# Sample tile before the prompt tiles, and every second of its v rows summed on VectorE

## The reference, cut to what matters

```python
h = layer_norm(ALPHA * x + token_mixer(x, ...))
# PEER(h): 8 heads x 16 best of 128 x 128 experts, for every token
s1, s2 = q1 @ keys1.T, q2 @ keys2.T         # q = h @ wq
expert, top_s = the 16 best of the sums of the 16 best of s1 and of s2
gate = softmax(top_s)
act  = gelu(einsum('td,thkd->thk', h, u[expert]))
out  = einsum('thk,thkd->td', gate * act, v[expert])
y = layer_norm(ALPHA * h + out)
```

## Time and profile before

| | |
|---|---|
| median of 3 runs | 2185.09 us |
| lowest and highest run | 2184.09 and 2194.29 us |
| span of the profiled execution | 2197.0 us |
| busy: PE, VectorE, ScalarE, GpSimd | 1744.4, 1086.9, 435.3, 843.3 us |
| bytes read, rate over the span | 550.23 MB, 256 GB/s |

### The profile page before, as it was taken

The page is one execution under the profiler, slowest core; times in us unless marked ns, Lnnn a source line. Parts: engine busy times, 40 slices in busy tenths (PEclk is TensorE's granted clock), DMA queues, the critical chain, the costliest instruction groups (busy, mean ns, idle before and its releaser), DMA issues.

```text
span 2197.0 us, 17908 instructions
## 1 busy us (share of the span) xinstructions
PE 1744.4 (79%) x5473; PEld 909.0 (41%) x5473; DVE 1086.9 (49%) x2606; ACT 435.3 (20%) x1031; POOL 843.3 (38%) x840
## 2 busy tenths in 40 slices
PE   7998888899888666787789778777989675766765
PEld 6844565444457222334445334333434222322322
DVE  3516456202147999535553645443142995343452
ACT  1211311201021111130332222114121122112111
POOL 0000000000003665554653554444143667777773
PEclk9999888999999988998889888889999988888888
DMA  6432011433359998996877897879898889999995
GB/s 203 168 137 105 8 70 54 178 134 115 133 171 339 351 315 285 335 375 226 276 267 276 298 314 253 274 264 372 288 388 288 311 311 345 368 361 353 364 363 224
DMA packets 220760, 563.39 MB, mean 256 GB/s; under 512 B 19770, under 2 KB 70394, under 8 KB 220250
## 3 DMA queue, kind: packets, MB, share of 16 engines
q0 software_dynamic: 112352, 408.88, 51.5%
q1 hardware_dynamic: 108050, 152.58, 20.3%
q10 hardware_dynamic: 288, 1.05, 0.1%
HBM read 550.23 MB, written 12.23 MB: 256 GB/s over the span
## 4 chain that ended last, share of the span: by engine, by line
PE 49%; DVE 19%; DMA 12%; issue 9%; POOL 5%; ACT 4%; another core or an unknown queue 1%; POOLq 0%; SPq 0%; DVEq 0%; ACTq 0%
PE bank L792 18%; PE bank L726 7%; PE bank L727 6%; PE bank L833 5%; DVE BIG L1489 4%; DMA wbuf<-in_w_in_dram 4%; ACT BIG L1164 3%; POOL BIG L658 3%; DMA out_s_ssm_dram<-BIG 3%; PE bank L772 2%; POOL BIG L653 2%; DMA BIG<-in_peer_v_dram,small 2%; PE bank L1104 2%; DMA BIG<-in_peer_u_dram,small 2%; DVE BIG L1947 2%
## 5 line engine op out<-in xcount | busy, mean ns | idle before, releaser
L726 PE MATMUL bank<-BIG 128*128 128x512 f32 x768 | 454.9, 677 | 267.5 <-DMA BIG<-in_peer_v_dram,small 117.6
L653 POOL DMA_INDIRECT BIG<-in_peer_u_dram,small x384 | 407.2, 1060 | 475.3 <-DVE small L1489 354.1
L658 POOL DMA_INDIRECT BIG<-in_peer_v_dram,small x384 | 409.1, 1065 | 194.6 <-issue 111.0
L792 PE MATMUL bank<-wbuf,BIG 128*128 128x512 f32 x992 | 435.1, 598 | 12.9 <-DMA wbuf<-in_w_in_dram 7.1
L727 PE MATMUL bank<-BIG 128*128 128x512 f32 x768 | 431.1, 645 | 0.0
L726 PEld LDWEIGHTS bank<-BIG 128*128 128x128 f32 x768 | 156.1, 215 | 488.1 <-issue 424.6
L1489 DVE CUSTOM_DVE_ANT_0 BIG<-BIG 128x1024 f32<-128x1024 f32 x256 | 303.9, 1221 | 14.4 <-DMA BIG<-in_peer_u_dram,small 12.6
L792 PEld LDWEIGHTS bank<-wbuf,BIG 128*128 128x128 f32 x992 | 189.1, 192 | 253.9 <-issue 235.0
L727 PEld LDWEIGHTS bank<-BIG 128*128 128x128 f32 x768 | 162.3, 211 | 216.1 <-issue 216.1
L2021 DVE CUSTOM_DVE_ANT_0 BIG<-BIG 128x1024 f32<-128x1024 f32 x128 | 156.3, 1226 | 182.5 <-DMA BIG<-in_peer_u_dram,small 137.0
L1164 ACT ACTIVATE BIG<-cst,small 128x128 f32<-128x128 f32 x384 | 127.7, 392 | 470.2 <-DVE small L1484 345.1
(11 more groups left out here) (186 smaller groups left out, 1274.8 us busy)
## 6 DMA issues: line engine op xcount, KB each, us to landing
wbuf<-in_w_in_dram SPq DMA_DIRECT2D x24, 2048.0 KB
wbuf<-in_w_in_dram SPq DMA_DIRECT2D x16, 1536.0 KB
wbuf<-in_w_ssm_br_dram SPq DMA_DIRECT2D x8, 2048.0 KB
wbuf<-in_peer_wq_dram SPq DMA_DIRECT2D x8, 2048.0 KB
wbuf<-in_w_attn_br_dram SPq DMA_DIRECT2D x4, 2048.0 KB
wbuf<-in_w_out_dram SPq DMA_DIRECT2D x4, 2048.0 KB
BIG<-in_state_ssm_dram SPq DMA_DIRECT2D x16, 512.0 KB, 6.1
out_s_ssm_dram<-BIG SPq DMA_DIRECT2D x16, 512.0 KB
```

The source lines that it names most:

```text
L653: pool.indirect_dma_start(slot, None, table_u, bass.IndirectOffsetOnAxis(ap=idx, axis=0)).then_inc(u_in[j], 16)
L658: pool.indirect_dma_start(slot, None, table_v, bass.IndirectOffsetOnAxis(ap=idx, axis=0)).then_inc(v_in[j], 16)
L726: mm(acc[0][:, :], dg[:, j, :], slots[j][:, 0:512], start=False, stop=False, skip_group_check=True)
L792: last = mm(dst[:, :], lhs(b, k, toks[t]), wbuf[b][:, k, :], start=(k == 0), stop=(k == KC - 1))
```

## The change

The order of the passes is turned: `ST` comes first, with nothing beside it, and `PR` second, with the 64 ticks of the sample tile's rows beside it (66 with the ends; 57 in the mixer, 8 beside the first pick of tile 0, one after). The rows of both prompt tiles, 2 x 128, then run alone in blocks of eight: 32 blocks instead of 16. The picks of tile 2 are beside the conv of `PR`; the first half of tile 0 is picked after `PR` with ticks beside it, the second half after the ticks, the halves of tile 1 after 4 and after 8 of the 32 blocks.

Of the two v rows of a tick the first stays on TensorE, and VectorE adds the second, times its weight, to a sum `accS` in SBUF (where a table lies that only the state-space part of `ST` reads); at the end the sum is added to the h of tile 2. ScalarE makes one diagonal a tick instead of two. The blocks of eight still use TensorE for all rows.

Also: the early gates are gone, all gates are done in their phase; small DMAs that GpSimd issued for `PR` (outputs, biases, norm weights) are issued by SyncE; the caches' loads come in the first conv; GpSimd reads the expert numbers where they lie, without copies, and its list and most loops are written out; `TICKS_AT` is new; the buffers lie elsewhere in SBUF.

```diff
-PROMPT_BLOCKS = 2 * BLOCKS
-TICKS = PROMPT_BLOCKS + 3
+TICKS = BLOCKS + 2
...
-TICKS_AT = dict(pick=1, conv=1, dt=1, qkv=1, tails=2, rope=1, keys=2, item1=2, item2=1, item3=1, ya=1,
-                select=1, xbt=2, seg=1, state=1, group=1, y=1, z=1, yT=1, ym=0, gates=1, mixedT=1, out=1, hT=1, wq=1,
-                scores=2)
+ORDER = {2: 0, 0: 1, 1: 2}
+
+TICKS_AT = dict(pick=(1,), conv=(1,), dt=(0,), qkv=(1, 0, 1, 1), tails=(0,), rope=(1,), keys=(1,), select=(1,),
+                item1=(0,), item2=(1, 0), item3=(0,), ya=(1,), xbt=(0,), seg=(0,), y=(1,), z=(1,), yT=(1,), ym=(1,),
+                gates=(1,), mixedT=(1,), out=(0, 1), hT=(1,), wq=(1, 0), scores=(0,))
...
             def tick(k):                                  # TensorE
...
-                    for j in range(b % 2 * WB, b % 2 * WB + WB):
-                        expert_rows(diag, v_used, j, vslot, (v_in[j], 16 * (b // 2 + 1)))
+                    j = b % 2 * WB
+                    expert_rows(2, diag, v_used, j, vslot, (v_in[j], 16 * (b // 2 + 1)))
...
-                if not q.streams:
-                    early_gates(0)
...
                 # ScalarE, conv of the second pass
-                        if q.streams and i >= 2 and j % 3 == 2:
+                        if not q.first and i >= 2 and j % 3 == 2:
                             step("pick")
...
             def tick(k):                                  # VectorE
...
+                b = k - 2
+                if b >= 0:
+                    slot = b % 2 * WB + 1
+                    dve.wait_ge(v_in[slot], 16 * (b // 2 + 1))
+                    if b:
+                        dve.wait_ge(v_added, b)
+                        stt(accS, vslot[slot], w8[b % 2][:, 1:2], accS, ALU.mult, ALU.add).then_inc(v_added, 1)
+                    else:
+                        tsc(accS, vslot[slot], w8[b % 2][:, 1:2], None, ALU.mult).then_inc(v_added, 1)
...
             # GpSimd
+            for b in range(BLOCKS + 2):
+                if b == BLOCKS // 2:
+                    pool.wait_ge(idx_ready, 2)
+                if b < BLOCKS:
+                    for j in range(b % 2 * WB, b % 2 * WB + WB):
+                        if b >= 2:
+                            pool.wait_ge(dot_done, WB * (b - 2) + j % WB + 1)
+                        gather(table_u, uslot[j], 2 * P + b * WB + j % WB, u_in[j])
+                c = b - 2
+                if c >= 0:
+                    for j in range(c % 2 * WB, c % 2 * WB + WB):
+                        if c >= 2:
+                            pool.wait_ge((v_used, v_added)[j % WB], c - 1)
+                        gather(table_v, vslot[j], 2 * P + c * WB + j % WB, v_in[j])
...
             # VectorE, the end
+            mixer(ST)
             mixer(PR)
-            mixer(ST)
+            pick(0, 0, lambda place: steps.at("pick"))
             places.append(list(steps.seen))
-            for half in range(2):
-                pick(2, half, lambda place: steps.at("pick"))
             steps.run(TICKS)
-
...
+            pick(0, 1, lambda place: None)
             finish(2)
...
+            blocks(0, 0, 4)
+            pick(1, 0, lambda place: None)
+            blocks(0, 4, 4)
+            pick(1, 1, lambda place: None)
+            blocks(0, 8, TURNS - 8)
+            blocks(1, 0, 2)
+            finish(0)
+            blocks(1, 2, TURNS - 2)
+            finish(1)
```

More of the change, by code:

```diff
@@ L534, in whole @@
                     pass
-            for q in (PR, ST):
-                if q.streams:
+            for q in (ST, PR):
+                if not q.first:
                     load_x(sp, q, q.x1, x_in)
@@ L854, in mixer @@
-                step("dt")
+                for half in range(8):
+                    b = half % 2
+                    loaded[b].take(pe)
+                    for j in range(3):
+                        dst = sbank()
+                        for k in range(KC):
+                            last = mm(dst[:, 0:q.tok], wbuf[b][:, k, j * P:(j + 1) * P], q.xT[:, k, :],
+                                      start=(k == 0), stop=(k == KC - 1))
+                        sf.give(last)
+                    if not q.first and half >= 4:
+                        step("pick")
@@ L856, in x_part, with time_steps @@
                 def x_part(b, k, tok):
                     return q.xT[:, k, tok]
-                products("qkv", 2, x_part, vf, vd, vbank)
+                def time_steps():
+                    phase("dt")
+                    pe.wait_ge(wdt_in, 16)
+                    pe.wait_ge(const_in, 32)
+                    for t in q.tiles:
+                        dst = sbank()
+                        for k in range(KC):
+                            last = mm(dst[:, 0:SH], q.xT[:, k, toks[t]], wdt[:, k, :], start=(k == 0), stop=(k == KC - 1))
+                        sf.give(last)
@@ new lines, in mixer @@
+                if q.first:
+                    time_steps()
+                    phase("qkv")
+                    products("qkv", 2, x_part, vf, vbank)
+                else:
+                    for _ in range(2):
+                        step("pick")
+                    time_steps()
+                    for _ in range(2):
+                        step("pick")
+                    phase("qkv")
+                    product("qkv", 0, x_part, vf, vbank)
+                    for _ in range(4):
+                        step("conv")
+                    product("qkv", 1, x_part, vf, vbank)
+                    for _ in range(4):
+                        step("conv")
+                    step("dt")
+                    for _ in range(2):
+                        step("qkv")
+                    products("qkv", 1, x_part, vf, vbank)
@@ L870, in mixer @@
                 step("rope")
-                def early_gates(b):
-                    loaded[b].take(pe)
-                    for t in q.tiles:
-                        dst = vbank()
-                        for k in range(KC):
-                            last = mm(dst[:, :], q.xT[:, k, toks[t]], wbuf[b][:, k, :], start=(k == 0), stop=(k == KC - 1))
-                        vf.give(last)
-                phase("early")
-                if not q.streams:
-                    early_gates(0)
                 phase("attention")
```

704 lines of the change are left out of this document (312 added, 392 removed).

## The result

The changed kernel takes 2231.8 us (median; 2228.6 to 2234.9) against 2184.6 for the kernel before on the same chip: a ratio of 1.024, with a 95% interval of 1.018 to 1.029. The profiled execution has a span of 2229.4 us. The forecast was 2225 and slower, with 2135 to 2300 as its range.

A forecast was written before the change was run, and what follows sets the result against it. Long stages were taken as bound by gathered bytes, the first by matmuls. Terms 546 + 853 + 97 + 741 gave 2237 us; with the profiled span 12 above the median, the forecast was 2225, 1.8% slower, range 2135 to 2300.

The forecast's parts named there:

- The likeliest case: Whole kernel: slower, the forecast 2225 us with its ends 2180 to 2260; chance 0.55.
- Stage A: Sample mixer with nothing beside it, at the start: 546 us, ends 500 to 590.
- Rival 2: Sample mixer runs cold, mostly at 1.2 GHz: it gains 64 us, total 2290; chance 0.12.
- Stage B: Prompt mixer with 57 ticks beside it: 853 us, ends 790 and 890, from a base of 649 without ticks.
- Rival 1: Prompt mixer: ticks fall into idle time, only TensorE's 98 us shows, stage 747, median 2119; chance 0.18.
- nearly even: Ticks beside the prompt mixer: moving the sum saves 31 us in product ticks, costs some 27 x 1.15 elsewhere.
- rival 4: Ticks: VectorE's sum frees nothing as TensorE waits for VectorE; 34 us more if product phases pay too, 2259; chance 0.10.
- Stage C: Between the prompt mixer and the steady tail, two selection halves and the sample tile's norm: 97 us.
- The tail's block, 22.4: Tail of 32 blocks of eight rows: the transfer at 374 GB/s sets 22.4 us a block, 672 for 30.
- Rival 3: Tail: without index copies GpSimd's 16 issues, 20 us, set the block; 72 less, 2153, needing 420 GB/s; chance 0.05.
- The picks of tile 1, 9 each: Two selections in the tail, 29 us each, one block of rows ahead: some 9 each, 18 together, ends 0 and 50.
- The 12 us: Whole kernel: profiled span stands 12 us above the median of the runs, so 2237 became 2225.

The follow-up runs named there:

- experiment 3: Kernel after with no tick beside the prompt mixer, all 66 after tile 0's first pick: 2389 us; kernel after with four conv ticks one half earlier: 2221.9 us.
- experiment 4: Kernel after with both v rows of a tick on TensorE: 2226.9 us; kernel before with GpSimd's list written out plus VectorE's sum: 2193.6 us.
- Experiment 1: Kernel before with GpSimd's list written out, no index copies: 2161.5 us; kernel after with the tail's gathers halved, dots shortened, or both: 2268.2, 2190.0, 2177.0 us.

## Why the prediction came out right, point by point

- **The sign and the size.** 2225 was forecast and 2231.8 measured. The likeliest case was the right one, with its mechanism: the mixers end some 305 earlier (315 forecast), the rest takes 337 more (355). That the total is off by only 7 is in part luck: in the tail 57 us too much for the blocks stand against 23 too little for the picks and some 26 in small terms.
- **Stage A.** 554 for 546, but of parts that miss both ways. Windows of conv, of rope to the end of attention, and of the state-space part:

```profile
15.00:78.00 63.00, 48.16 (x386) 47.42 (x386) 32.06 (x92) 6.48 (x23) 0.00 (x0) 0.92 0.83 268
...
109.00:207.00 98.00, 72.51 (x509) 60.11 (x507) 43.50 (x88) 22.01 (x57) 0.00 (x0) 0.76 0.08 29
...
222.00:378.60 156.60, 109.24 (x478) 66.67 (x477) 74.85 (x196) 25.56 (x44) 0.00 (x0) 0.84 0.42 121
```

  Conv took 63, not 54: TensorE waited 9.7 for one weight load, which stands behind the caches' loads in SyncE's queue. Rope, keys and attention took 98 for 77, the state-space part 157, near the 162 of its chain, where I took 172. From z to the scores it is 175, as worked out.
- **Rival 2, the cold sample mixer,** did not come: the granted clock of stage A is 0.87. It was near in one part, attention with 0.76, which was also the part that ran 21 over.
- **Stage B** was 2 us off. That is luck as well: by experiment 3 the stage without ticks is 675 and not 649, since VectorE waits for ScalarE in the second pick without any tick, and the ticks cost 186 and not 204, 3.3 each. Rival 1, ticks in idle time, needed B under 812 and is out.
- **The sum on VectorE, "nearly even",** is shown by experiment 4, and with it rival 4 is out for the product phases. The step behind it, 1.72 of TensorE saved for each tick, failed: 41 of the 98 us didn't come, with the granted clock at 0.79 instead of 0.91 and 0.89.
- **Stage C** was 103 for 97; the empty time of the DMA queue was 26.65 for 25.
- **The tail's block, 22.4, is the step that failed.** I took the 0.99 share of the DMA engines and 374 GB/s for the transfer's limit. Experiment 1 shows that it was GpSimd's list there, and that the transfer's limit is 410 GB/s, 20.48 for a block: 57 us less over 30 blocks. Rival 3 named the mechanism, issues without index copies (though not that the transfer would stop the gain at 20.48), and gave it 0.05 because "no long stretch shows" the rate it needs. The rate that a queue reaches when its issuer is slow says nothing of what it can do. The Trainium skill, "DMA: Bandwidth & Descriptors", section "Specifications", has 358 GB/s as a core's share of HBM, which I weighed; the same skill's "HBM Reference", section "Specifications (TRN2)", says that a core streaming alone measures about 425, and the 410 here stands on that side.
- **The picks of tile 1, 9 each,** were mis-sized: 20.5. The 10 us by which they exceed one block's cover was right; the slow issues after them, another 10, were missing. The prediction had the rule for it, the contention of two-input VectorE instructions with GpSimd, and dismissed it by the median of 949 ns. A median over 384 issues does not show how many are held; in the tail of before the mean was 1.034 us, and the same row's longest, 3152, might have made me look.
- **The 12 us** that I took off because the profiled execution of before lay above its median: the profiled execution of after lay at its median. The sum, 2237, would have been 5 us above the measured time, the forecast was 7 below.

## What to carry to other kernels

Before a stage is called bound by its transfers, look at the issuing engine's timeline: rows with "issue" as the only reason for idle time, and a sum of issues near the block's time, say that the list may be the limit whatever the DMA share says. They don't prove it: the kernel after shows the same rows at 20.48, and there it took runs with a shorter list, half the bytes and short dots to tell the limits apart. Work that has to stand between two stages that stream (a selection here) is best cut into steps that fit the consumer's idle time in each block. And work moved from one engine to another is paid in full wherever the receiver sets the pace: price the move stage by stage.

## What the runs showed of the hardware that I had not expected

- A gather of 128 rows costs GpSimd 0.94 us and 0.30 between two, for rows of 4 KB and of 2 KB alike; at 2 KB that caps the gathers at some 206 GB/s (experiment 1).
- An issue that begins while VectorE takes a dot over 128x1024 lasts 0.81 us and what is left of that dot, up to 1.99 in all (204 of 205 in the tail of the kernel after). One that begins between dots takes 0.94. In steps of 1.28 both fit, with the issue at 0.98.
- The mean share of the DMA engines is 0.97 to 0.99 at 364 and 374 GB/s and 1.03 at 410, so it does not tell a full queue from one that is nearly kept busy; with rows half as long it is 0.66 at 187 GB/s.
- Taking every second v row from TensorE lowered its granted clock in the old order from 0.90 to 0.80 over 1036 us, with no change in when the stage ended.
